# Hybrid attention with two heads at a time: 64-row score tiles, 64-column value tiles, and each stage behind a gate product

## The reference, cut to what matters

```python
def hybrid_layer(x, ...):
    h = rmsnorm(x, norm_mix_g)
    q, k, v, u_pool, gate_logits = split(h @ w_in)        # 512, 512, 512, 512, 2048 columns
    q = apply_partial_rotary(rmsnorm(heads(q), q_norm_g), pos)
    k = apply_partial_rotary(rmsnorm(heads(k), k_norm_g), pos)
    attn = softmax(q @ k.T * 64 ** -0.5, causal) @ v      # 8 heads
    pooled = multiscale_pool_mixer(u_pool, w_pool, pool_scale)
    gates = sigmoid(gate_logits + b_gate)                 # two of width 1024
    mixed = gates[0] * (attn @ w_branch_attn) + gates[1] * (pooled @ w_branch_pool)
    x = x + mixed @ w_out
    ...                                                   # feed-forward part
```

## Time and profile before

| | |
|---|---|
| median of 3 runs | 1185.75 us (1185.22 to 1185.87) |
| the profiled execution's own time | 1185.63 us |
| its span, first to last instruction | 1183.7 us |
| PE busy, share of the span | 1144.8 us, 97% |
| DVE busy | 748.3 us, 63% |
| ACT busy | 604.8 us, 51% |
| mean granted TensorE clock | 0.994 |

### The profile page before, as it was taken

The page is one execution under the profiler, slowest core; times in us unless marked ns, Lnnn a source line. Parts: engine busy times, 40 slices in busy tenths (PEclk is TensorE's granted clock), DMA queues, the critical chain, the costliest instruction groups (busy, mean ns, idle before and its releaser), DMA issues.

```text
span 1183.7 us, 18050 instructions
## 1 busy us (share of the span) xinstructions
PE 1144.8 (97%) x6724; PEld 1029.8 (87%) x6724; DVE 748.3 (63%) x1097; ACT 604.8 (51%) x895; POOL 59.6 (5%) x49
## 2 busy tenths in 40 slices
PE   6999999999899999999989999999989999999998
PEld 6997888888789999999967888888988899999987
DVE  5976655653765557656457555554766575998970
ACT  6435644453455544554347554544545474666650
POOL 0100000000000000000000000000020020222210
PEclk9999999999899999999999999999999999999999
DMA  8555655765174466434334756673524454555670
GB/s 266 172 183 163 213 173 182 244 235 160 50 199 111 121 159 159 121 83 115 106 117 132 240 168 205 225 252 93 154 91 157 130 174 154 183 179 178 222 257 18
DMA packets 215381, 193.74 MB, mean 164 GB/s; under 512 B 9577, under 2 KB 190877, under 8 KB 215325
## 3 DMA queue, kind: packets, MB, share of 16 engines
q1 hardware_dynamic: 215325, 192.97, 52.5%
HBM read 191.88 MB, written 1.05 MB: 163 GB/s over the span
## 4 chain that ended last, share of the span: by engine, by line
PE 92%; DVE 4%; ACT 3%; issue 0%; DMA 0%; SPq 0%; DVEq 0%; ACTq 0%
PE ps L648 13%; PE ps L650 13%; PE ps L649 13%; PE ps L593 7%; PE ps L595 7%; PE ps L594 7%; PE ps L723 6%; PE ps L725 6%; PE ps L724 6%; PE ps L755 3%; PE ps L776 2%; DVE w_lo L1575 2%; PE ps L769 2%; PE ps L672 1%; PE ps L778 1%; PE ps L823 1%
## 5 line engine op out<-in xcount | busy, mean ns | idle before, releaser
L1575 DVE TENSOR_TENSOR w_lo<-raw,w_hi 128x1024 fp32r<-128x1024 f32 (+2 forms) x314 | 422.8, 1391 | 114.8 <-ACT w_hi L1146 114.5
L1146 ACT ACTIVATE w_hi<-raw 128x1024 fp32r<-128x1024 f32 (+2 forms) x314 | 354.1, 1173 | 110.0 <-PE ps L650 28.5
L593 PE MATMUL ps<-x_hi,w_hi 128*128 128x256 f32 x656 | 187.7, 286 | 3.4 <-DVE w_lo L1575 3.4
L595 PE MATMUL ps<-x_hi,w_lo 128*128 128x256 f32 x656 | 186.4, 284 | 0.0
L594 PE MATMUL ps<-x_lo,w_hi 128*128 128x256 f32 x656 | 186.3, 284 | 0.0
L648 PE MATMUL ps<-w_hi,x_hi 128*128 128x512 f32 (+1 forms) x368 | 145.1, 394 | 0.3 <-issue 0.3
L650 PE MATMUL ps<-w_hi,x_lo 128*128 128x512 f32 (+1 forms) x368 | 142.7, 388 | 0.0
L649 PE MATMUL ps<-w_lo,x_hi 128*128 128x512 f32 (+1 forms) x368 | 142.5, 387 | 0.0
L593 PEld LDWEIGHTS ps<-x_hi,w_hi 128*128 128x128 f32 x656 | 126.6, 193 | 3.9 <-DVE w_lo L1575 3.8
L594 PEld LDWEIGHTS ps<-x_lo,w_hi 128*128 128x128 f32 x656 | 126.6, 193 | 0.1
L595 PEld LDWEIGHTS ps<-x_hi,w_lo 128*128 128x128 f32 x656 | 126.5, 193 | 0.0
(11 more groups left out here) (218 smaller groups left out, 1755.8 us busy)
## 6 DMA issues: line engine op xcount, KB each, us to landing
raw<-in_ffn_w_gate_up SPq DMA_DIRECT2D x176, 256.0 KB, 4.2
raw<-in_w_kv SPq DMA_DIRECT2D x96, 256.0 KB, 4.7
raw<-in_w_up SPq DMA_DIRECT2D x44, 512.0 KB, 4.5
raw<-in_ffn_w_down SPq DMA_DIRECT2D x24, 768.0 KB, 5.9
raw<-in_conv_w_in SPq DMA_DIRECT2D x24, 512.0 KB, 5.0
raw<-in_w_q SPq DMA_DIRECT2D x48, 256.0 KB, 4.1
raw<-in_w_in SPq DMA_DIRECT2D x20, 512.0 KB, 4.4
raw<-in_w_down SPq DMA_DIRECT2D x12, 768.0 KB, 5.7
```

The lines of the kernel that those rows point to most:

```text
L593: nc.tensor.matmul(o, wh[:, k0 + k, c], hi[:, k, :], start=(k == 0), stop=False)
L595: ins = nc.tensor.matmul(o, wl[:, k0 + k, c], hi[:, k, :], start=False, stop=(k == kt - 1))
L1146: nc.scalar.activation(w_hi[:, s, a * ph.cols:b * ph.cols], src, ACT.Copy)\
L1575: nc.vector.tensor_tensor(w_lo[:, s, c], src, w_hi[:, s, c], ALU.subtract)\
```

## The change

Two heads of a pair are done together. `qT2` and `kT2` become one tile `qk2` without the zeros: ACT's "store" is 2 copies in place of 6, and GpSimd's memset of `kT2` is gone. The scores of head 0 run on rows 0 to 63 and those of head 1 on rows 64 to 127, alternating, into banks 4 and 6; the values alternate between output partitions 0 to 63 and 64 to 127 of bank 5. `prob2`, `probT2` and the small softmax columns have a copy for each head of the pair. "Turn", and "values" with the next "scores", stand behind different gate chunks: scores(0) after 118, turn(0) after 119, values(0) and scores(1) after `w_pool`, turn(r) after 121, 123, 125, values(r) and scores(r+1) after 122, 124, and values(3) after 126. Nothing of attention is left in `branches`. `hybrid_turn(2)` moves behind chunk 117's last product, and on DVE w_lo of chunk 119 moves ahead of `hybrid_qkv(3)`. In `w_pool`, DVE makes w_lo of chunk 122 after the softmax of pair 1; in `gates_a`, w_lo of 120 comes after the softmax of pair 0.

```diff
-        qT2 = at("qT2", [P, 4, T], F32, b + 16384)
-        kT2 = at("kT2", [P, 2, 4, T], F32, b + 20480)
+        qk2 = at("qk2", [P, 2, 4, T], F32, b + 16384)
...
-        prob2 = at("prob2", [P, 384], F32, y_at + 4096)
-        probT2 = at("probT2", [P, 384], F32, y_at + 5632)
+        prob2 = at("prob2", [P, 2, 384], F32, b + 24576)
+        probT2 = at("probT2", [P, 2, 384], F32, y_at + 4096)
...
+        PAIR_S, PAIR_O = (4, 6), 5
+        SOFT2 = ((2, 4, 6, 10), (32, 34, 36, 38))
...
+            def pair_scores(r):
+
+                if r > 0:
+                    pe.wait_ge(prob_stored, HEADS + 2 * r)
+                for qt in range(2):
+                    c, w = tok(qt), P * (qt + 1)
+                    for hh in range(2):
+                        f = slice(hh * HD, (hh + 1) * HD)
+                        ins = nc.tensor.matmul(ps[:, PAIR_S[hh], qt * P:qt * P + w], qk2[f, 0, r, c], qk2[f, 1, r, 0:w],
+                                               start=True, stop=True, skip_group_check=True)
+                        if qt == 1:
+                            ins.then_inc(scored, 1)
+
+            def pair_turn(r):
+
+                for hh in range(2):
+                    pe.wait_ge(prob_set, HEADS + 2 * r + hh + 1)
+                    turn_probs(prob2[:, hh], PAIR_S[hh] * 512, 1)
+
+            def pair_values(r):
+
+                pe.wait_ge(prob_stored, HEADS + 2 * r + 2)
+                if r > 0:
+                    pe.wait_ge(o_split, 8 + r)
+                for kt in range(2):
+                    for hh in range(2):
+                        f = slice(hh * HD, (hh + 1) * HD)
+                        ins = nc.tensor.matmul(ps[f, PAIR_O, kt * P:T], v2[:, kt, r, f],
+                                               probT2[:, hh, kt * T:kt * T + T - kt * P], start=(kt == 0),
+                                               stop=(kt == 1), skip_group_check=True)
+                        if kt == 1:
+                            ins.then_inc(head_done, 1)
...
# PE, gates_a
-                            wait_emptied(pe, by_name["qkv2b"], j, 0)
-                            hybrid_step(j)
+                            if j == 0:
+                                wait_emptied(pe, by_name["qkv2b"], 0, 0)
+                                pair_scores(0)
+                            else:
+                                pair_turn(0)
# PE, qkv2b
-                            if j == 1 and t == 0:
-                                hybrid_turn(2)
+                    hybrid_turn(2)
# PE, w_pool
+                    wait_emptied(pe, by_name["qkv2b"], 1, 0)
+                    pair_values(0)
+                    pair_scores(1)
# PE, gates_b
-                        hybrid_step(l + 2)
+                        r = l // 2 + 1
+                        if l % 2 == 0:
+                            pair_turn(r)
+                        else:
+                            pair_values(r)
+                            if r < 3:
+                                pair_scores(r + 1)
# PE, branches
-                    hybrid_head(7, "turn")
-                    pe.wait_ge(max_set, HEADS + 8)
                     pool_part(ph, 1)
-                    hybrid_head(7, "values")
# ACT, store
-                        nc.scalar.activation(qT2[:, k, c], ps[:, bank, 0:P], ACT.Copy)
-                        for hh in range(2):
-                            r = slice(hh * HD, (hh + 1) * HD)
-                            ins = nc.scalar.activation(kT2[r, hh, k, c], ps[r, bank, P:2 * P], ACT.Copy)
+                        ins = nc.scalar.activation(qk2[:, :, k, tok(t)],
+                                                   ps[:, bk + 4 * t, 0:256].rearrange("p (w c) -> p w c", w=2), ACT.Copy)
# ACT, w_pool, behind the four copies to p_hi
+                    hybrid_part("output", 0)
+                    hybrid_part("exp", 1)
                     ahead(ph, 0, 0, split, 3)
# DVE, qkv2b
                         if r == 3:
                             pool_means()
+                            ahead(ph, 1, 0, split, 2)
                         hybrid_qkv(r)
-                        ahead(ph, r - 2, 0, split, 2)
+                        if r == 2:
+                            ahead(ph, 0, 0, split, 2)
# DVE, gates_a
                         gate_logits(ph, l, 2 * l)
+                        if l == 0:
+                            pair_max(0)
+                            pair_normalise(0)
                         ahead(ph, l, 0, split, 2)
-                        hybrid_step(l)
# DVE, w_pool
-                    ahead(ph, 0, 0, split, 2)
+                    pair_max(1)
...
+                    pair_normalise(1)
+                    ahead(ph, 0, 0, split, 2)
# DVE, gates_b
                         gate_logits(ph, l, 4 + 2 * l)
+                        if l % 2 == 0:
+                            head_out(r - 1)
+                        elif r < 3:
+                            pair_max(r + 1)
+                            pair_normalise(r + 1)
+                        else:
+                            head_out(3)
                         ahead(ph, l % 4, l // 4, split, 2)
-                        hybrid_step(l + 2)
-                    hybrid_step(8)
# GpSimd
-                        nc.gpsimd.memset(kT2[:], 0.0).then_inc(zeroed, 1)
```

More of the change, by code:

```diff
@@ L488, in build @@
         HEADS = 16
+        PAIR_S, PAIR_O = (4, 6), 5
+        SOFT = (2, 4, 6, 10)
+        SOFT2 = ((2, 4, 6, 10), (32, 34, 36, 38))
         def load_vectors(eng, g, signal):
@@ L1401, in hybrid_part @@
                     act.wait_ge(v_stored, 8 + k + 1)
[L1402 to L1403 removed]
                     for t in range(2):
[L1405 to L1409 removed]
+                        ins = nc.scalar.activation(qk2[:, :, k, tok(t)],
+                                                   ps[:, bk + 4 * t, 0:256].rearrange("p (w c) -> p w c", w=2), ACT.Copy)
                     ins.then_inc(emptied[bk], 1)
                 elif what == "exp":
[L1412 removed]
+                    for hh in range(2):
+                        softmax_exp(prob2[:, hh], (slice(0, P), slice(P, 384)), HEADS + 2 * k + hh, SOFT2[hh])
                 elif what == "turned":
[L1414 to L1415 removed]
+                    for hh in range(2):
+                        act.wait_ge(prob_turned, HEADS + 2 * k + hh + 1)
+                        nc.scalar.activation(probT2[:, hh], ps[:, PAIR_S[hh], 0:384], ACT.Copy).then_inc(prob_stored, 1)
                 else:
                     act.wait_ge(head_done, HEADS + 2 * k + 2)
[L1418 to L1426, removed]
+                    nc.scalar.activation(t_hi[:, k, :], ps[:, PAIR_O, 0:T], ACT.Copy).then_inc(o_hi, 1)
             def sigmoid(c):
@@ L1755, in up_conv_body, with masked_max @@
                 return body
-            def masked_max(src, mask, parts, c):
+            def masked_max(src, mask, parts, c, at_=SOFT):
                 dve.wait_ge(scored, c + 1)
@@ L1885, in gate_logits, with pair_max, pair_normalise @@
                                         by_token(rstd), ALU.mult).then_inc(emptied[s], 1)
-            def head_front(hd):
-                masked_max(prob2, mask1, ((slice(0, P), 4 * 512), (slice(P, 384), 4 * 512 + P)), HEADS + hd)
-                normalise(prob2, (slice(0, P), slice(P, 384)), HEADS + hd)
-            def hybrid_step(hd):
-                if hd < 8:
-                    head_front(hd)
-                if hd > 0 and hd % 2 == 0:
-                    head_out(hd // 2 - 1)
+            def pair_max(r):
+                for hh in range(2):
+                    s0 = PAIR_S[hh] * 512
+                    masked_max(prob2[:, hh], mask1, ((slice(0, P), s0), (slice(P, 384), s0 + P)), HEADS + 2 * r + hh,
+                               SOFT2[hh])
+            def pair_normalise(r):
+                for hh in range(2):
+                    normalise(prob2[:, hh], (slice(0, P), slice(P, 384)), HEADS + 2 * r + hh, SOFT2[hh])
             def pool_means():
@@ L1916, in head_out @@
                 dve.wait_ge(o_hi, 8 + r + 1)
-                nc.vector.tensor_tensor(t_lo[:, r, :], ps[:, 6, 0:T], t_hi[:, r, :], ALU.subtract).then_inc(o_split, 1)
+                nc.vector.tensor_tensor(t_lo[:, r, :], ps[:, PAIR_O, 0:T], t_hi[:, r, :], ALU.subtract).then_inc(o_split, 1)
             def emit(ph):
```

34 lines of the change are left out of this document (22 added, 12 removed).

## The result

The changed kernel takes 1169.91 us (median of 4 runs, 1169.56 to 1172.36), the kernel before on the same chip 1185.53 us (4 runs, 1185.22 to 1185.87). The ratio is 0.9873, 95% interval 0.9861 to 0.9885: 15.6 us less. The forecast was 1172.9 us with a range of 1170.5 to 1178.3. The profiled execution took 1169.99 us; its span is 1168.2 us, 15.5 us shorter than the 1183.7 before.

The account below looks back on a forecast made before the run. PE's own work and the few gaps in its stream bound the kernel. Gains 1.5 + 3.4 + 1.6 + 5.2 + 1.3 + 4.2 less 0.7, 3.3 and 0.4 give 12.8 us: 1172.9 us, range 1170.5 to 1178.3.

Parts of the forecast that it names:

- The turn of pair 2: hybrid_turn(2) moved from the middle of chunk 117 to behind it: PE's wait for rotated q and k is covered, +1.5 us.
- The wait before 119 and its half clock: w_lo of chunk 119 moved ahead on VectorE: PE's wait (+3.4 us) and the half clock behind it (+1.6) go.
- The gate product between turn and values: A gate product stands where PE waited for ScalarE's copies: 0.74 us for each of 7 heads (+5.2), head 7 +1.3.
- The cost of scores and values: Two heads' products partly overlap: values 1.03, scores 1.01 us a pair, against 1.58 and 1.52 without overlap; +4.2 us.
- The new waits: Start-up around w_pool: PE waits 0.6 us for pair 0's copies, 0.8 in turn(1), 1.9 for w_lo of 122; -3.3.
- w_lo of 128: At the end, w_lo of chunk 128 stands behind head_out(3) on VectorE: -0.4 us.
- Changes of shape: Some four more changes of tile shape around scores and values, at 0.15 to 0.17 us each: -0.7 us.
- A: Rival: no overlap of the two heads in scores and values; 1175.4 us, chance 2 in 10.
- B: Rival: start-up waits more, through half clock (1.6 us) or a later load (1.0); 1174.5 to 1175.5 us, 1.5 in 10.
- C: Rival: each of 24 tile changes in scores and values costs a 0.16 us drain, no overlap; 1179.3 us, 1 in 10.
- D: Rival: slower than before, tile changes in scores and values costing 0.53 us each; 1188 us, 0.4 in 10.
- E: Rival: no measurable change, tile changes near 0.4 us each or later stages giving the gain back; 1185 us, 0.5 in 10.

Follow-up runs that it names:

- turn_mid: Changed kernel with hybrid_turn(2) back in the middle of chunk 117; 1170.36 us, ratio 0.9868.
- lo_late: Changed kernel with VectorE's w_lo of chunk 119 back behind hybrid_qkv(3); 1170.65 us, ratio 0.9876.
- before_sched: Kernel before with two moves alone: hybrid_turn(2) behind chunk 117, w_lo of 119 ahead of hybrid_qkv(3); 1183.82 us against 1185.66.
- turn_values: Changed kernel with turn and values adjacent again for pairs 1 to 3, behind chunks 122, 124 and 126; 1175.98 us, ratio 0.9919.
- head_by_head: Changed kernel with scores and values issued for one head of a pair, then the other, not alternating; 1171.58 us, ratio 0.989.
- same_rows: Changed kernel with head 1's scores also taken from rows 0 to 63, so head 0's twice (different result); 1171.96 us, ratio 0.9885.
- hi_behind: Changed kernel with ScalarE's w_hi of chunk 122 moved behind the exponentials of pair 1; 1167.31 us, ratio 0.9847.

## Why the prediction was right and where it was wrong

**What bounds the kernel** was read rightly. What was gained is PE idle time removed, half clock avoided, or PE instructions that share time, and behind the stage nothing was given back (231.44 and 231.37 us).

**The turn of pair 2** (+1.5) measured 1.56. **The wait before 119 and its half clock** (3.4 + 1.6, less 0.25) measured 4.77 of 4.75. But the terms are no sum of independent parts, as the forecast treated them. *turn_mid* and *lo_late* undo them one at a time and the stretch stays within 0.3 and 0.1 us of the changed kernel's, because the idle stretch before 122 takes up either; *before_sched* has them without the rest and wins 1.8 of 6.5, as another wait takes the place of theirs.

**The gate product between turn and values** (7 x 0.74 + 1.3) is borne out: no wait for probT stands in the waits of the changed kernel, and putting a separation back costs 0.90 us in each of the pairs 2 and 3 (*turn_values*). For a pair that is less than twice 0.74: the pair would have had one wait where the two heads had two, so of this term about 0.6 a pair belongs to the pairing and 0.9 to the separation.

**The cost of scores and values** is the step that failed: "each f32 product is two instructions in the same tile, so in this order only the second of one head and the first of the other can share time". The forecast's 1.03 and 1.01 us a pair measured 0.80 and 0.85, of which about 0.1 is the switch to the next shape. The two halves of the array run as if each had a queue of its own (*head_by_head*), and only as long as they are different halves (*same_rows*). The full halving that the Trainium skill's pages "TensorE: Matmul & The Clock Gate", part 3, and "TensorEngine Tiling (Array Packing)", Overview, describe is what the trace shows: 0.80 and 0.85 against 0.79 and 0.76 for one head, where one half alone needs 1.51. The first page's rule that such products also start in program order does not agree with *head_by_head*. Size of the miss: 4 x 0.23 for the values and 4 x 0.16 for the scores, 1.6 us. Only 3 x 0.23 and 2 x 0.16, 1.0 us, lie behind the idle stretch before chunk 122 and reach the end; the rest PE spends waiting there.

**The new waits** (-3.3). The 0.6 us for probT of pair 0 did not happen: values start at 884.70, 0.28 behind the last product of `w_pool`, of which 0.12 is its step and 0.16 the change of shape. The other two were forecast at 0.8 and 1.9 us. From 892.2, where chunk 121 ends, to 895.80 pass 3.6 us, of which the turn is 0.66: 2.9 of idle for 2.7 forecast, with the mechanism as forecast (ScalarE at the transfer of 122, p_hi behind it, w_lo of 122 last) and shown by *hi_behind*. But when chunk 122 starts is set by that chain and not by PE: 46.7 us behind the turn of pair 1 (849.08 to 895.80), where the forecast had 47.55 (849.95 to 897.5). VectorE was done with w_lo of 120 0.4 us earlier than forecast, and from there to the end of w_lo of 122 passed 12.9 us for 13.4, of which 5.1 for 5.4 until the transfers of 122 were in. w_lo of 128 was 0.3 with its restart for 0.4.

**Changes of shape** (-0.7) at 0.15 to 0.17 each: the ones in the profile are 0.16 (884.42 to 884.70), and 0.1 where scores give way to a gate product. Gate chunk 122 to 124 took 14.03 us (895.80 to 909.83) for 14.3.

So the 15.50 us of span gained are 2.7 more than the sum: 0.87 from where these two executions stood when they came to the stage, 0.83 because chunk 122 could start earlier, 0.93 between there and the first product over t_hi (41.03 us for 41.96), nearly the 1.0 of the overlap, and 0.07 behind it. The wait of 0.6 us that did not happen, and the overlap of pair 0 and of scores(1), are no terms of their own: they lie ahead of chunk 122. Whether the medians share the 0.87 is open: seven variants and the changed kernel's two profiles put that place anywhere in 1.8 us, and it is chance, no part of the mechanism.

**The rivals.** A (no overlap) is what *same_rows* builds for the scores, and its signs are absent from the changed kernel. B happens, but not in each execution: one of the two profiles of the changed kernel has the half clock, at 2.6 us where B said 1.6. The range ended at 1170.5 us, 0.6 above the measured median; in the profiled execution each of the three parts of the miss (0.87, 0.83, 0.93) is larger than what was wanting (0.5), so with any one of them as forecast the time would have been inside. C and D fell with the price of a tile change, E with the branches' 17.6 us.

## What to carry to other kernels

In this kernel small products in different halves of the array (64 rows or 64 columns, f32, 128 to 256 columns long) shared nearly all their time, alternating or one head after the other, so pair the heads even where the program issues them one after the other; but give the engine that must copy between two such stages a long product of other work to hide in. When several gains lie ahead of one wait on another engine, they don't add: find that wait first (here it was ScalarE standing at a transfer with urgent work behind it, 2.6 us), move it, and then count the others.

## What the hardware showed that I had not expected

- Instructions of the two halves start out of program order: in *head_by_head* the other head's first starts 14 ns behind this head's first, ahead of three that the program has before it.
- A change of half costs nothing that shows within a pair (8 instructions in 0.85 us with three changes, 0.86 with one), a change of shape between stages 0.10 to 0.16 us.
- The length of the waits alone does not decide the clock: 0.50 and 1.72 us around a turn left it at 1.00, and so did 0.69 and 1.72 in *head_by_head*, while behind 0.61 and 1.72 in another execution it was 0.50. A single wait of 2.18 us left it at 1.00 (*lo_late*, 1.00 in each stretch of 3 us from 878 to 887); behind one of 2.35 and one of 3.45 it was 0.50.
